# Attention on rounded halves, issued step by step between the projection's groups, with three weight slots

## The reference: what is computed

```
z = rmsnorm(x) @ w_in                      # q, k, v, qi, ki, wi, u, gv: 2088 columns
score = sum_h relu(qi_h . ki) * wi_h       # 8 index heads of 32
keep the top 128 keys of each row (48 for the later tokens), chunk-causal
a = softmax(q . k / 8 over the kept keys) @ v     # 8 heads of 64 on 2 key heads
b = gelu(u) * (W_s @ rmsnorm(gelu(gv)) + b_s)     # 8 groups, blocks of 128 positions
x += [a | b] @ w_out;   x += relu(rmsnorm(x) @ w1)^2 @ w2
```

## Time and profile before

| | us |
|---|---|
| three runs | 1504.86, 1506.54, 1445.23 (median 1504.86) |
| the profiled execution | 1423.3 |
| its span | 1421.4 |
| PE, DVE, ACT, POOL busy | 1396.3, 663.6, 518.5, 186.1 |
| mean granted TensorE clock | 0.972 of full |

### The profile page before, as it was taken

One profiled execution on the slowest core, in us unless ns is written; L12 is line 12 of the kernel. 1 busy time (PEld: TensorE's weight loads), 2 busy tenths in 40 slices (PEclk: granted clock), 3 DMA queues, 4 the chain that ended last, 5 costly groups with the idle time before them and its releaser, 6 DMA issues.

```text
span 1421.4 us, 22280 instructions
## 1 busy us (share of the span) xinstructions
PE 1396.3 (98%) x9329; PEld 1271.9 (89%) x9329; DVE 663.6 (47%) x1172; ACT 518.5 (36%) x956; POOL 186.1 (13%) x215
## 2 busy tenths in 40 slices
PE   6999999999999999999999999999999999999997
PEld 5767777999999999999976677689999999999997
DVE  5258733354444444444533793434544444443443
ACT  6266544333123123123334753533321322322322
POOL 4246300110000000000204550002000000000011
PEclk9999879999999999999999995999999999999999
DMA  6212200232323232222331121003232222323221
GB/s 181 84 46 60 78 5 1 60 88 76 89 75 90 76 88 83 82 80 85 105 89 46 45 74 34 5 16 89 75 89 80 85 86 78 87 77 90 75 60 67
DMA packets 169252, 102.37 MB, mean 72 GB/s; under 512 B 6920, under 2 KB 159424, under 8 KB 169152
## 3 DMA queue, kind: packets, MB, share of 16 engines
q1 hardware_dynamic: 169152, 100.94, 24.6%
HBM read 96.98 MB, written 3.95 MB: 71 GB/s over the span
## 4 chain that ended last, share of the span: by engine, by line
PE 92%; DVE 6%; ACT 1%; DMA 1%; POOL 1%; issue 0%; SPq 0%; POOLq 0%; DVEq 0%; ACTq 0%
PE bank L1338 65%; PE bank L1109 11%; PE bank L1223 4%; PE bank L1259 3%; DVE late L866 2%; PE bank L1239 2%; DVE m L864 2%; PE bank L1129 1%; PE bank L1274 1%; PE bank L1290 1%; DMA late<-in_x_prompt 1%; PE bank L1204 1%; POOL late L480 1%; PE bank L1144 1%; PE bank L1357 0%
## 5 line engine op out<-in xcount | busy, mean ns | idle before, releaser
L522 ACT ACTIVATE ring_hi<-ring_raw 128x1024 fp32r<-128x1024 f32 x176 | 184.8, 1050 | 306.0 <-PE bank L1338 248.7
L1338 PE MATMUL bank<-vh,ring_hi 128*128 128x288 f32 x1280 | 276.9, 298 | 0.0
L1338 PE MATMUL bank<-vl,ring_hi 128*128 128x288 f32 x1280 | 276.2, 297 | 0.0
L1338 PE MATMUL bank<-vh,ring_lo 128*128 128x288 f32 x1280 | 276.2, 297 | 0.0
L767 DVE TENSOR_TENSOR ring_lo<-ring_raw,ring_hi 128x1024 fp32r<-128x1024 f32 x164 | 214.7, 1309 | 126.3 <-ACT ring_hi L522 119.4
L1338 PE MATMUL bank<-xh,ring_hi 128*128 128x288 f32 x1024 | 220.8, 297 | 0.1
L1338 PE MATMUL bank<-xl,ring_hi 128*128 128x288 f32 x1024 | 220.2, 296 | 0.0
L1338 PE MATMUL bank<-xh,ring_lo 128*128 128x288 f32 x1024 | 220.2, 296 | 0.0
L1338 PEld LDWEIGHTS bank<-vh,ring_hi 128*128 128x128 f32 x1280 | 206.5, 190 | 0.0
L1338 PEld LDWEIGHTS bank<-vh,ring_lo 128*128 128x128 f32 x1280 | 206.4, 189 | 0.0
L1338 PEld LDWEIGHTS bank<-vl,ring_hi 128*128 128x128 f32 x1280 | 206.3, 190 | 0.0
(11 more groups left out here) (161 smaller groups left out, 1495.5 us busy)
## 6 DMA issues: line engine op xcount, KB each, us to landing
ring_raw<-in_w_ff SPq DMA_DIRECT2D x128, 512.0 KB, 4.1
ring_raw<-in_w_in SPq DMA_DIRECT2D x32, 512.0 KB, 3.7
ring_raw<-in_w_out SPq DMA_DIRECT2D x16, 512.0 KB, 4.2
late<-in_x_prompt SPq DMA_DIRECT2D x4, 512.0 KB, 6.0
out_y_prompt<-late SPq DMA_DIRECT2D x4, 512.0 KB, 2.7
w_sp<-in_w_spatial SPq DMA_DIRECT2D x2, 512.0 KB, 4.3
gate_bc<-in_gate_norm SPq DMA_DIRECT2D x2, 256.0 KB, 6.2
out_k_prompt<-z SPq DMA_DIRECT2D x2, 256.0 KB, 4.3
```

The source lines that it names most:

```text
L522: s.activation(ring_hi[:, n % NSLOT, :], ring_raw[:, n % NRAW, :], ACT.Copy).then_inc(hi_ready, 1)
L1338: last = mm(bank[2 * (u % 4) + half][:, 0:HALF], w[:, k, :], a[:, k, HALVES[half]], start=k == order[0] and w is wh and a is ah, stop=k == ...
```

## The change

1. `NSLOT` goes from 4 to 3: a slot of halves is split again as soon as PE has finished the block three before.
2. Attention is no stage of its own. Its pieces have group numbers (`QK_AT`, `T_AT`, `QT_AT`, `MIX_AT`, `INV`): they stand between the groups of the gate and u columns, g = 45 to 79, and in slots 80 to 85 behind them. `fill(g)` says how many top-key steps DVE takes in a slot; ahead of the first masked logits of a tile it takes all that this tile still needs (`while done[tile] < total_steps(tile)`).
3. Logits, probabilities by values and queries by keys are made on rounded halves: three matmuls each. A logits step takes 4, 2, 2, 1 or 1 heads at once (26 steps, all in bank 5). A value step takes four heads and one block of 128 keys (24 steps): four transposes, then three matmuls of 512 columns (256 for SMP) that produce the result already transposed. So DVE gets new subtractions (`q_low`, `p_low`, `out_low`) and ACT new roundings (`q_high`, `p_high`, `out_high`).
4. The division by the row's sum moves from DVE behind the value product to POOL ahead of the transposes (`normalise`).
5. For tile 1 and SMP the scaling and adding of the index heads moves from ACT and POOL to one DVE instruction a head.
6. Spatial mixing takes two groups of channels for four tiles at once. `w_out` is loaded in three pieces, so that its rows match the new order of heads, and units 0 to 2 take their attention half first. The eight `w_out` units use the banks in reverse order.

```diff
-    NRAW, NSLOT = 2, 4
+    NRAW, NSLOT = 2, 3
...
+    QT_AT = {IDX0 + 24 + a: a for a in range(NT)}
+    QK_AT = [IDX0 + 25 + k for k in range(10)] + [IDX0 + 40 + k for k in range(8)] + [IDX0 + 50 + k for k in range(8)]
+    T_AT = {}
+    for k, (g, b) in enumerate(STEPS):
+        T_AT[max([QK_AT[QK_OF[GQA * g + GQA - 1]] + 3, *(x + 1 for x in T_AT)])] = k
...
+    def fill(g):
+        d = g - IDX0
+        return (0 if d < 9 else 2 if d < 13 else 4 if d < 24 else 1 if d < 29 else 2 if d < 35 else 4 if d < 40 else
+                2 if d < 48 else 4 if d < 50 else 0)
...
+                    if at in QK_IN:
+                        tile = TILE_ORDER[QK[QK_IN[at]][0]]
+                        if QK[QK_IN[at]][1] == 0 and tile:
+                            while done[tile] < total_steps(tile):
+                                topk_next(at)
+                            dve.wait_ge(dve_step, step_of[tile])
+                        for i in step_items(QK_IN[at]):
+                            masked_logits(i)
...
+                for at in range(END):
+                    n, t = divmod(at, NT)
+                    if n < S_OUT:
...
+                        group(n, t, w)
...
+                    if at in QK_IN:
+                        scores_step(QK_IN[at])
+                    if at in T_AT:
+                        p_transpose(T_AT[at])
+                    if at - 1 in T_AT:
+                        weighted(T_AT[at - 1])
```

More of the change, by code:

```diff
@@ L35, in hybrid_encoder_program @@
     NH = DA // HD
+    GQA = NH // NKV
     NIH = 8
@@ L553, in _ @@
             act.wait_ge(g_ready, 1)
-            for n in range(NSLOT):
-                if n:
+            for n in range(KT // 2):
+                if 0 < n < NSLOT:
                     split_hi(n)
@@ L718, in _ @@
+                    if at in QT_AT:
+                        q_high(QT_AT[at])
+                    if at in T_AT:
+                        p_high(T_AT[at])
+                g = NGR - 1
+                out_high(g)
+                for a in range(NT):
+                    mt_copy(a)
                 for j in range(KT):
@@ new lines, in mt_low @@
+                def mt_low(a):
+                    t = U_ORDER[a]
+                    dve.wait_ge(vh_ready, (NT + FT) * l + a + 1)
+                    v.tensor_tensor(vl[:, KT // 2:KT, cols(t)], bank[t][:, 0:4 * ROWS[t]].rearrange("p (k n) -> p k n", k=4),
+                                    vh[:, KT // 2:KT, cols(t)].bitcast(F32), ALU.subtract).then_inc(vl_ready, 1)
+                for at in range(END):
+                    n, t = divmod(at, NT)
+                    if t == 0 and 1 <= n <= S_OUT and n + NSLOT - 1 not in POOL_SPLITS:
@@ new lines, in scores_step @@
+                def scores_step(k):
+                    a = QK[k][0]
+                    t, first = TILE_ORDER[a], step_items(k)[0]
+                    pe.wait_ge(q_lo_ready, NT * l + a + 1)
+                    if k == 0:
+                        pe.wait_ge(idx_relu, NX * (l + 1))
+                    else:
+                        pe.wait_ge(masked, NI * l + first)
+                    if QK[k] == (NT - 1, 0):
+                        pe.wait_ge(mix_evac, NT * l + MIX_BANK.count(5))
+                    kh, kl = (ks_hi, ks_lo) if t == SMP else (k_hi, k_lo)
+                    for i in step_items(k):
+                        hh, S = ITEMS[i][1], KEYS[t]
+                        b = HD * (hh // GQA)
+                        for m, kk in ((q_hi, kh), (q_hi, kl), (q_lo, kh)):
+                            last = mm(bank[5][0:ROWS[t], (i - first) * S:(i - first + 1) * S], m[b:b + HD, hh % GQA, cols(t)],
+                                      kk[b:b + HD, 0:S], start=m is q_hi and kk is kh, stop=m is q_lo)
+                    last.then_inc(qk_done, 1)
@@ new lines, in weighted @@
+                def weighted(k):
+                    g, b = STEPS[k]
+                    a = g // NKV
+                    t = TILE_ORDER[a]
+                    n = min(P, KEYS[t] - b * P)
+                    block = b if t != SMP else (NT, SMP)[b]
+                    pe.wait_ge(p_lo_ready, NS * l + k + 1)
+                    if k == 0:
+                        pe.wait_ge(v_ready, l + 1)
+                        pe.wait_ge(q_lo_ready, NT * (l + 1))
+                    if b == 0 and g:
+                        pe.wait_ge(al_ready, NGR * l + g)
+                    for w, p in ((v_hi, p_hi), (v_lo, p_hi), (v_hi, p_lo)):
+                        last = mm(bank[7][:, 0:GQA * ROWS[t]], w[0:n, block, :], p[0:n, k % 2, 0:GQA * ROWS[t]],
+                                  start=b == 0 and w is v_hi and p is p_hi, stop=b == BLOCKS[a] - 1 and p is p_lo)
+                    last.then_inc(o_step, 1)
```

819 lines of the change are left out of this document (455 added, 364 removed).

## The result

The changed kernel takes **1448.7 us** (median of 20 runs, 1445.7 to 1455.0). Twenty runs of the kernel before on the same chip have a median of 1447.9 and reach from 1413.1 to 1506.5. Taken over the runs within 1.5% of each kernel's fastest, which are all twenty of the changed kernel but only two of before's (1413.1 and 1413.3), the ratio is **1.0258, with a 95% interval of 1.0223 to 1.0292: slower**. Median against median, the two kernels are equal. My profiled sum was 1406 and my median 1488; the profiled execution took 1448.1 (span 1446.3), 24.8 more than the profiled one of before, where I expected 17 less.

A forecast was written before the change was run, and what follows sets the result against it. PE, busy for 98% of the span, was taken as the bound. Layer gains of 11.6 and 7.2 us less 2 for reversed banks gave -17 on 1423.3: 1406 profiled, 1488 median with the difference carried over; range 1405 to 1530.

The forecast's parts named there:

- the loss to the clock: Groups 62 to 67, behind the pause at slot 61: half clock costs between 0 and 7 us, taken as 3.
- PE's own list: PE's work in a layer up to its first unit: about 181 us against 229.6 in the kernel before.
- the 82 us: Whole kernel: the unexplained difference between profiled execution and median of runs, carried over unchanged to the changed kernel.
- my 218 us for layer 1: Layer 1, first group to first unit: the stretches sum to 218 us where 229.6 stand, 11.6 less.
- rival 2: Attention stage: the runs' unexplained 82 us are its low clock and go with it; about 1415; chance 0.12.
- A gap of 8 us: Slot 61: PE stands about 8 us for DVE's masks, with a piece of half clock behind it.
- PE unbroken in g 68 to 79: Groups 68 to 79: PE has 36 us of work, the other engines are light; 37 us taken.
- Units at 6.4 us: Products: units still 6.4 us, no wait for `ring_lo` with three slots, one wait of 1 us at unit 8.
- g 35 to 44 in 25.5 us: Groups 35 to 44: PE 20.6 us, POOL 24, PE tied by three index-head buffers; 25.5 us.
- Rival 3: Interleaved slots: the PSUM ring makes PE wait and the clock fall; about 1464 profiled, 1546 median; chance 0.17.
- Rival 4: g 26 to 44 and slot 61: waits eat the gain; within 10 us of 1505; chance 0.10.
- The rule weighed: Groups 62 to 67: DVE and POOL exclude each other in SBUF; up to 5 x 1.0 us a layer, not taken.

The follow-up runs named there:

- e1_three_slots: The kernel before with three weight slots instead of four, nothing else changed: 1506.5 us, beside 1451.3 for the kernel before.
- e8_delay: The kernel before, four slots, with seven more top-key maxima on VectorE behind the last projection group: 1510.8 us, ratio 1.0607.
- e12_slots_hold: The kernel before with three slots and tile 3's last six top-key steps held back until the attention's masks: 1498.5 us, ratio 1.0322.
- e11_hold: The kernel before, four slots, with tile 3's last six top-key steps held back until the attention's masks: 1496.3 us, ratio 1.0332.
- f4_balance: The changed kernel with tile 3's index adds on VectorE, top keys dealt out otherwise, transposes, gate mean and norms in other slots: 1421.6 us, ratio 1.0022 to before.
- e2_no_lump: The changed kernel without tile 2's remaining top-key steps ahead of its first masks in slot 61: 1437.0 us.

## Why the prediction was wrong

**Two terms of the layer's sum failed: the loss to the clock, 3 us where 13 were measured, and PE's own list, 181 us where 195 were measured.** A third step, the 82 us carried over to the median, failed as well.

In its parts my 218 us for layer 1 were PE's list, 181, waits of 34 over it, and 3 for the clock. Measured: 195, 30 and 13. The waits, which I had to guess slot by slot, came out 4 us too high in all. The list was 14 us short, the clock's loss 10, so a layer that I had 11.6 us shorter than before came out 8 longer.

- *Half clock, 3 us.* I charged it to one place, behind slot 61. It fell five times in a layer, for 34 us, each time in or behind a wait of 1.6 to 9.6 us.
- *PE's list, 181 us.* I priced groups, logits and values at the pace of a long run of equal matmuls, 0.233 us for 512 columns. Added up from the starts in the trace of layer 1 (idle time left out, half-clock time counted at half), the groups take 119.9 us where I had 112, the logits 21.6 for 18 and the value products 18.2 for 15; the other lines are within 1 us together. The kernel before has 115.6 for its groups, so half of the groups' miss was there to be read. The timeline of the changed kernel, slot 71, at full clock (a group's last matmul, a logits step, the next transposes; then the end of a value step and the next group):

```profile
920.33 0.40 PE L1284 MATMUL bank<-ring_hi,xl 128*128 128x512 f32 x1
920.66 0.50 PE L1391 MATMUL bank<-k_hi,vh 64*128 64x512 f32 x1
921.00 0.39 PE L1391 MATMUL bank<-k_lo,vh 64*128 64x512 f32 x1
921.23 0.39 PE L1391 MATMUL bank<-k_hi,vl 64*128 64x512 f32 x1
921.55 0.33 PE L1416 MATMUL bank<-ident,pl_b 128*128 128x128 f32 x1
...
925.39 0.39 PE L1439 MATMUL bank<-p_lo,v_hi 128*128 128x512 f32 x1
925.62 0.39 PE L1284 MATMUL bank<-ring_hi,xh 128*128 128x512 f32 x1
```

The group's last start to the first logit is 0.33 us and not 0.23; the three logits take 0.34, 0.23 and 0.32, 0.89 where I had 0.70. The logits use 64 rows and the groups 128, and passing from one to the other costs 0.1 us each way. It isn't every change of kind that costs: from a value product to the next group it is 0.23 us, as within a group. The earlier trace rows had the cost: 0.33 us from the group's last matmul (119.43) to the index pair of 32 rows (119.76). What the rest of the 14 us is made of I haven't shown.

The third step is the median. I carried the 82 us between profile and median over to the changed kernel, and gave rival 2 (the excess is the clock of the attention, and goes with it) 0.12, because "attention's own list of some 72 us would cost less than half of that" at half clock. That was worked out for one layer. Two layers of 72 us doubled are up to 144, less what the profile has already; e1_three_slots and e8_delay have 269.5 and 269.6 us of attention where the profile of before has 179.6, 90 more, and the medians of before lie between. So the excess did go: the changed kernel's median is its profile. Rival 2's mechanism was right, and its time (1415) fell short by 34 us, the misses of the layer's sum.

That 1448.7 lies inside my range is luck: a profile 42 us over my sum, less an excess of 82 us that never came.

Point by point:

- *A gap of 8 us, ended by DVE's masks, half clock behind it*: 9.6 us, and 10.3 at half clock. Right.
- *DVE over 95% busy from there back to g 56*: 25.8 of the 26.9 us up to the masks (863.3 to 890.2). Right.
- *PE unbroken in g 68 to 79*: 0.7 us idle, but 42.1 us for my 37: list and clock again.
- *Units at 6.4 us, no wait for `ring_lo`, 1 us at unit 8*: right, and e12_slots_hold against e11_hold shows no cost of the third slot.
- *g 35 to 44 in 25.5 us*: 29.8. I had counted POOL's three blocks of work and not their order: rotation in one piece ahead of the adds that PE's third pair needs.
- *Rival 3*, the only slower one, was the ring of each slot. The ring was mild: PE idle for 3.0 us in g 45 to 55 and 0.7 in 68 to 79. Its sign, half clock between g 45 and 55, did come (829.2 to 836.0), but behind the wait of q's transposes and not from the ring; as a sign it was badly chosen. The time came out slower than the two best runs of before for another reason, the pauses at four hand-overs of lists, and the clock.
- *Rival 4*, the gain eaten by waits: against before's median of twenty (1447.9, not the 1504.9 I had) its outcome is what came, and its two places, g 26 to 44 and slot 61, hold 15 of the 30 us idle.
- *The rule weighed.* In the changed kernel the mean of the gate's squares, five numbers a row, took 1.92 us on DVE (0.14 in the kernel before) while POOL split a weight block:

```profile
877.09 1.92 DVE L1131 TENSOR_SCALAR mv<-ssv 128x5 f32<-128x5 f32 x1 [0.85 <-ACT late L709]
```

```profile
876.59 2.39 POOL L574 TENSOR_TENSOR ring_lo<-ring_raw,ring_hi 128x1024 fp32r<-128x1024 f32 x1 [7.60 <-ACT ring_hi L632]
```

It ends 0.03 us behind POOL's instruction. A gate norm, two SBUF inputs, took 2.66 us instead of 0.75 beside the next split:

```profile
898.26 2.66 DVE L1047 SCALAR_TENSOR_TENSOR late<-late,rv,gate_bc 128x512 f32<-128x512 f32 x1
```

The line's eight large pieces, where the earlier trace rows has 6.0 us and 746 ns:

```profile
L1047 DVE SCALAR_TENSOR_TENSOR late<-late,rv,gate_bc 128x512 f32<-128x512 f32 x8 | 9.7, 1219 | 0.0
```

PE waited 1.6 us for the masks behind that norm. The Trainium skill, SBUF — State Buffer, section "SBUF: two separate sides", has a VectorE instruction with two SBUF inputs, or in a perf mode that takes two ports, and a GpSimd one exclude each other for a whole instruction. The trace agrees for the norm; the mean has one SBUF input, and no run shows in which mode it ran. I had up to 5 us a layer by the rule and took none. One of the five norms of a layer was held up, and the others took 0.73 to 0.75 us. DVE lost 3.7 us a layer in all (1.8 and 1.9), both times ahead of masks that PE waited for. In f4_balance the mean takes 1.05 us and stands behind tile 2's second masks, and the wait of 4.2 us is gone; the run doesn't tell the shorter mean from its new place.

## What to carry to other kernels

Write the time of a stretch as work at full clock, idle time and loss to the clock, each from the windows, before you forecast it: the profiles here differ in all three, and the medians are equal. Work that is interleaved in small pieces pays for every place where one engine's list stands in the wrong order, far more than for the added changes between kinds of matmul (2 us a layer here); look at which list the wait ends in, and move that one item. And where runs of a kernel scatter by several per cent, find the stretch whose clock differs before saying what a change is worth: here the same list took 88 or 132 us.

## What the runs showed of the hardware

- **A busy PE at half clock.** In e1_three_slots PE was busy by the profile for 74.0 of 74.0 us of plain float32 attention at clock 0.50. The Trainium skill, TensorE: Matmul & The Clock Gate, section "Part 1: The HAM clock gate", says that "the default state is throttled, and activity releases the throttle". The trace doesn't agree as far as busy time is activity: matmuls of 64 to 512 float32 columns with no idle time between them in the profile did not release it there, while groups of 512 columns on halves kept 1.00 through 95 us.
- **Same list, two times.** Attention of one layer took 87.8 to 91.8 us in three stretches of the kernel before and 131.6 in a fourth, with equal waits. With six top-key steps moved on VectorE and no wait at its head it took 124 to 131 in both layers.
- **Into the logits and out again.** Between matmuls of 512 columns on 128 rows and such on 64 or 32 rows the start came 0.1 us later (0.33 instead of 0.23 us); from a value product to a group, or from a group to transposes, all on 128 rows, it did not.
- **A shorter pause, the same fall.** With 3.1 us instead of 9.6 at the same logits (e2_no_lump) the clock fell at the same point of the layer, and 31 us of it instead of 34 were at half level.
